# A hybrid recurrent decoder step: mixer started on the residual not yet normed, gate rows and stabiliser moved ahead of other tiles, and the third branch's division folded into its head norm

## The reference

```
rmsnorm(x, g) = x * rsqrt(mean(x*x) + 1e-6) * g
x = x + 0.5 * (silu(gate) * up) @ w_down        # gate, up = split(rmsnorm(x, g) @ w_up)
z = rmsnorm(x, mix_norm) @ w_in                 # all inputs of the three branches and their gates
x = x + (sum over branches of sigmoid(gate_c) * (o_c @ w_branch_c)) @ w_out
```

```
h = num / max(|den|, exp(-m_t))                     # one den and one m per token and head
o = h * rsqrt(mean(h*h over the head) + 1e-6) * g * sigmoid(mo)
```

## Time and profile before

| | us |
|---|---|
| median of 3 runs | 3288.1 (3286.03 to 3306.51) |
| profiled execution, whole | 3299.21 |
| its span | 3297.3 |
| PE busy in it | 3149.6 (96%) |
| mean granted TensorE clock | 0.964 of full |

### The profile page before, as it was taken

The page is one execution under the profiler, slowest core; times in us unless marked ns, Lnnn a source line. Parts: engine busy times, 40 slices in busy tenths (PEclk is TensorE's granted clock), DMA queues, the critical chain, the costliest instruction groups (busy, mean ns, idle before and its releaser), DMA issues.

```text
span 3297.3 us, 63200 instructions
## 1 busy us (share of the span) xinstructions
PE 3149.6 (96%) x23984; PEld 3044.7 (92%) x23984; DVE 1375.0 (42%) x1545; ACT 521.5 (16%) x789; POOL 1630.9 (49%) x908
## 2 busy tenths in 40 slices
PE   8999989898999999999999999989989999999998
PEld 8999989888888799999999998989888888999997
DVE  4232544535323574232642326364363254832326
ACT  2010012130231211010120101121302312110101
POOL 5555644333332366565665556533333323665655
PEclk9999989999988899999999999999999988999999
DMA  3222231131211232222222222311312122322222
GB/s 122 89 85 88 96 111 64 51 101 58 81 57 62 64 122 85 89 83 90 92 88 90 89 84 95 111 58 55 103 58 73 59 64 74 117 83 90 89 89 92
DMA packets 115154, 276.30 MB, mean 84 GB/s; under 512 B 9240, under 2 KB 53152, under 8 KB 114720
## 3 DMA queue, kind: packets, MB, share of 16 engines
q1 hardware_dynamic: 65088, 237.01, 21.6%
q10 hardware_dynamic: 49888, 36.71, 3.6%
HBM read 255.16 MB, written 18.52 MB: 83 GB/s over the span
## 4 chain that ended last, share of the span: by engine, by line
PE 85%; DVE 9%; issue 4%; ACT 1%; POOL 1%; DMA 0%; ACTq 0%; DVEq 0%; PEld 0%; POOLq 0%; PEldq 0%
PE dense L366 72%; PE SA L560 1%; PE SA L495 1%; PE SB L570 1%; PE SA L574 1%; PE SA L481 1%; PE SA L547 1%; DVE sst L1214 1%; DVE rows L1004 1%; DVE tmp L1201 1%; PE SA L424 1%; DVE vblk L1207 1%; PE SA L550 1%; POOL Wl L346 0%; PE SA L466 0%
## 5 line engine op out<-in xcount | busy, mean ns | idle before, releaser
L344 POOL TENSOR_SCALAR Wh<-raw 128x1024 fp32r<-128x1024 f32 x452 | 489.7, 1083 | 1609.9 <-PEq L371 1604.2
L346 POOL TENSOR_TENSOR Wl<-raw,Wh 128x1024 fp32r<-128x1024 f32 x452 | 1141.0, 2524 | 37.7
L366 PE MATMUL dense<-Hh,Wh 128*128 128x272 f32 x3872 | 837.7, 298 | 29.5 <-DVE Hl L913 13.4
L366 PE MATMUL dense<-Hh,Wl 128*128 128x272 f32 x3872 | 818.7, 294 | 0.0
L366 PE MATMUL dense<-Hl,Wh 128*128 128x272 f32 x3872 | 818.3, 294 | 0.0
L366 PEld LDWEIGHTS dense<-Hh,Wh 128*128 128x128 f32 x3872 | 629.3, 194 | 39.3 <-DVE Hl L926 15.2
L366 PEld LDWEIGHTS dense<-Hl,Wh 128*128 128x128 f32 x3872 | 628.9, 195 | 0.0
L366 PEld LDWEIGHTS dense<-Hh,Wl 128*128 128x128 f32 x3872 | 623.6, 195 | 0.0
L366 PE MATMUL dense<-Ah,Wh 128*128 128x272 f32 x1408 | 291.9, 289 | 6.7 <-DVE Al L948 4.2
L366 PE MATMUL dense<-Mh,Wh 128*128 128x272 f32 x1408 | 290.2, 288 | 1.8 <-DVE X L1318 1.8
L366 PE MATMUL dense<-Ml,Wh 128*128 128x272 f32 x1408 | 291.1, 288 | 0.0
(11 more groups left out here) (312 smaller groups left out, 2958.4 us busy)
## 6 DMA issues: line engine op xcount, KB each, us to landing
raw<-wst SPq DMA_DIRECT2D x452, 512.0 KB, 3.2
x_keep<-X ACTq DMA_DIRECT2D x2, 2176.0 KB, 7.8
X<-x_keep ACTq DMA_DIRECT2D x16, 272.0 KB, 3.6
sst<-st_h ACTq DMA_DIRECT2D x8, 512.0 KB, 4.1
s_h<-sst ACTq DMA_DIRECT2D x8, 512.0 KB, 3.1
sst<-st_c ACTq DMA_DIRECT2D x8, 512.0 KB, 3.9
s_c<-sst ACTq DMA_DIRECT2D x8, 512.0 KB, 3.1
X<-xT ACTq DMA_DIRECT2D x4, 544.0 KB, 7.6
```

The costliest lines, as they stand in the source:

```text
L344: pool.tensor_scalar(Wh[:, j, :], raw[:, j, :], 1.0, 0.0, ALU.mult, ALU.add).then_inc(glink, 1)
L346: pool.tensor_tensor(Wl[:, j, :], raw[:, j, :], f32(Wh[:, j, :]), ALU.subtract).then_inc(glink, 1)
L366: mm = pe.matmul(dps[slot][:, a, 0:HALF], w[:, ring, w0:w0 + 128], x[:, k, a * HALF:(a + 1) * HALF], start=(k == 0 and n == 0), stop=(k == ...
```

## The change

Three edits stand together.

1. **The seam.** In the last third of the first half-step ACT and DVE also make `Mh`/`Ml` of the residual scaled by the mixer's g (8 instructions each). PE computes tiles 0 to 3 from these, with the sum over the partitions (`rms`) behind tile 0. DVE multiplies each of the four by `rs` as it reads it out, ACT makes its sigmoid from the product, and DVE multiplies the two. The normed residual `Hh`/`Hl`, which the other tiles need, is made by DVE and ACT between these (`mix_norm`).
2. **The order.** The small tile is tile 4, directly behind `hq`; then come `hi` (5 to 8), `hf` (9 to 12) and `hg` (13 to 16). Step `rows` stands after tile 5, the stabiliser after tile 6, and `exps` and `cols` after tile 12. The first six steps of the first scan are woven with tiles 13 to 20.
3. **The third branch.** The head norm cancels a common factor of num, so the division is left out: ACT squares den and exp(-m), each scaled by sqrt(eps), squares num and copies it out; DVE takes the maximum of the two squares and adds it, capped, to num squared; the norm then has 1e-36 in place of eps. The weight of step `o` in `weave` is 5 instead of 8.

```diff
-HQ, HF, HI, HG, SMALL, GQ, GK, GV, GG = 0, 4, 8, 12, 16, 17, 19, 21, 25
+HQ, SMALL, HI, HF, HG, GQ, GK, GV, GG = 0, 4, 5, 9, 13, 17, 19, 21, 25
...
-        s += [(("o", br, h), 8 if br == 2 else 4), (("z", br, h), 8)]
+        s += [(("o", br, h), 5 if br == 2 else 4), (("z", br, h), 8)]
...
-    return (group(0, HG) + weave(group(HG, SMALL + 1), scan0[:6], 0)
-            + [("rows", 0, 0), ("stab", 0, 0)] + group(GQ, GV) + [("exps", 0, 0), ("cols", 0, 0)]
+    return (group(HQ, HI + 1) + [("rows", 0, 0)] + group(HI + 1, HI + 2) + [("stab", 0, 0)] + group(HI + 2, HG)
+            + [("exps", 0, 0), ("cols", 0, 0)]
+            + weave(group(HG, GV), scan0[:6], 0)
...
-                rms(L * 3 + 1)
...
+                        if n < SMALL:
+
+                            tile(L, n, Mh, Ml, first=(pre_lo, L * KT) if n == 0 else None)
+                            if n == 0:
+                                rms(L * 3 + 1)
+                            continue
...
+            def mix_norm(L):
+
+                def hi(k):
                     act.wait_ge(norm_h, L * KT + (k + 1))
                     act.activation(Hh[:, k, :], tmp[:, k % 2, :], ACT.Copy).then_inc(norm_hi, 1)
+
+                def sig(t):
+                    if t > 1:
+                        act.wait_ge(hq_mul, L * SMALL + (t - 1))
+                    act.wait_ge(slot_free[t % 2], ONE + L * (TILES // 2) + ((MIX_T0 + t) // 2 + 1))
+                    act.activation(tmp[:, 4 + t % 2, :], R0[0][:, t, :], ACT.Sigmoid).then_inc(sig_done, 1)
+
+                for t, ks in enumerate(((0, 1), (2, 3, 4), (5, 6, 7), ())):
+                    sig(t)
+                    for k in ks:
+                        hi(k)
...
-                    ch.did(act.activation(tmp[:, 3, 0:SEQ], SA[:, 0, :], ACT.Copy))
+                    ch.did(act.activation(tmp[:, 3, 0:SEQ], SA[:, 0, :], ACT.Square, scale=ROOT_EPS))
...
-                        act.activation(tmp[:, 5, 0:SEQ], SB[:, 0, :], ACT.Abs).then_inc(d_abs, 1)
+                        act.activation(tmp[:, 5, 0:SEQ], SB[:, 0, :], ACT.Square, scale=ROOT_EPS).then_inc(den_sq, 1)
...
+                        act.activation(tmp[:, 2, 0:SEQ], SA[:, 0, :], ACT.Square).then_inc(num_sq, 1)
...
+                    ch.did(act.activation(O[:, h, 0:SEQ], SA[:, 0, :], ACT.Copy))
...
+                dve.wait_ge(rs_ready, n + 1)
+                hq_scale(0)
+                h(0); h(1); lo(0)
+                hq_gate(0); hq_scale(1)
+                h(2); lo(1); h(3); lo(2); h(4); lo(3)
+                hq_gate(1); hq_scale(2)
+                h(5); lo(4); h(6); lo(5); h(7); lo(6); lo(7)
+                hq_gate(2); hq_scale(3)
+                hq_gate(3)
...
-                        dve.wait_ge(d_abs, (L * HEADS + h) * 2 + 2)
+
+                        dve.wait_ge(den_sq, (L * HEADS + h) * 2 + 2)
                         ch.link(TT(nb, nb, tmp[:, 5, :], ALU.max))
-                        ch.link(dve.reciprocal(nb, nb))
-                        ch.did(TT(O[:, h, 0:SEQ], SA[:, 0, :], nb[:, 0:SEQ], ALU.mult))
-                        ch.did(TT(O[:, h, SEQ:TOK], SA[:, 1, 0:SMP], nb[:, SEQ:TOK], ALU.mult))
-                        ch.sync()
-                        ch.did(TT(tmp[:, 2, :], O[:, h, :], O[:, h, :], ALU.mult))
+                        dve.wait_ge(num_sq, (L * HEADS + h) * 2 + 2)
+                        ch.link(STT(tmp[:, 2, :], nb, HUGE, tmp[:, 2, :], ALU.min, ALU.add))
```

More of the change, by code:

```diff
@@ L36 @@
 EPS = 1e-6
+ROOT_EPS = 1e-3
+TINY = 1e-36
+HUGE = 1e37
 FF_BLOCK = 8
@@ L129, in piece_of, with dram_piece @@
     return t
+def dram_piece(p):
+    i = p - MIX_P0
+    if i == SMALL:
+        return MIX_P0 + 16
+    if HI <= i < HF:
+        return MIX_P0 + 8 + i - HI
+    if HF <= i < HG:
+        return MIX_P0 + 4 + i - HF
+    if HG <= i < GQ:
+        return p - 1
+    return p - 1 if TWICE < p < FFN2_P0 else p
 class Chain:
@@ L323, in _, with run, listed @@
             with sp.Fori(0, DEPTH) as L:
-                with sp.Fori(0, TWICE // 2) as it:
-                    for j in range(2):
-                        load(L * PIECES + j + it * 2, L * PIECES + j + it * 2, j)
-                for p in range(TWICE, FFN2_P0):
-                    load(L * PIECES + p, L * PIECES + (p if p == TWICE else p - 1), p % 2)
-                with sp.Fori(0, FFN_TILES // 2) as it:
-                    for j in range(2):
-                        load(L * PIECES + (FFN2_P0 + j) + it * 2, L * PIECES + (FFN2_P0 + j) + it * 2, j)
+                def run(p0, p1):
+                    with sp.Fori(0, (p1 - p0) // 2) as it:
+                        for j in range(2):
+                            load(L * PIECES + (p0 + j) + it * 2, L * PIECES + (p0 + j) + it * 2, j)
+                def listed(p0, p1):
+                    for p in range(p0, p1):
+                        load(L * PIECES + p, L * PIECES + dram_piece(p), p % 2)
+                run(0, MIX_P0 + SMALL)
+                listed(MIX_P0 + SMALL, MIX_P0 + GQ + 1)
+                run(MIX_P0 + GQ + 1, TWICE)
+                listed(TWICE, FFN2_P0)
+                run(FFN2_P0, PIECES)
         @block.gpsimd
@@ L590, in _ @@
                     elif what == "tile":
-                        tile(L, n, Hh, Hl, first=(norm_lo, (L * 3 + 1) * KT) if n == 0 else None,
+                        if n < SMALL:
[3 more added lines that the diff above has]
+                            continue
+                        tile(L, n, Hh, Hl, first=(norm_lo, (L * 3 + 1) * KT) if n == SMALL else None,
                              part=1 if m else None)
@@ L650, in ffn, with scaled_hi @@
                         use = L * (TILES // 2) + (t0 + off + 2 * nf + m) // 2 + 1
-                        scaled_hi(Hh, m, 0, m % 2, use)
-            def scaled_hi(dst, m, g0, slot, use):
+                        scaled_hi(Hh, m, 0, m % 2, use, norm_hi)
+                else:
+                    for m in range(KT):
+                        use = L * (TILES // 2) + (t0 + off + 2 * nf + m) // 2 + 1
+                        scaled_hi(Mh, m, PG["mix"], m % 2, use, pre_hi)
+            def scaled_hi(dst, m, g0, slot, use, done):
                 act.wait_ge(slot_free[slot], ONE + use)
                 act.activation(dst[:, m, :], X[:, m, :], ACT.Copy,
-                               scale=par[:, g0 + m:g0 + m + 1]).then_inc(norm_hi, 1)
+                               scale=par[:, g0 + m:g0 + m + 1]).then_inc(done, 1)
             def tile_wait(L, t):
@@ L665, in tile @@
                 free = slot_free[slot]
-                if t in range(HQ, HF) or t in range(HG, SMALL) or t in range(GG, G0[0]):
+                if t in range(HG, GQ) or t in range(GG, G0[0]):
                     tile_wait(L, t)
@@ L670, in tile @@
                     act.activation(halves(tmp[:, t % 2, :]), ps, ACT.Sigmoid).then_inc(sig_done, 1)
-                elif t in range(HF, HI):
+                elif t in range(HF, HG):
                     tile_wait(L, t)
@@ L850, in _ @@
                     if s[0] == "tile":
-                        tile(L, s[1])
+                        if s[1] >= SMALL:
+                            tile(L, s[1])
                         if s[1] == G0[0]:
```

87 lines of the change are left out of this document (50 added, 37 removed).

## The result

The changed kernel takes **3234.06 us** (median of 4 runs, 3229.72 to 3243.32), the kernel before 3290.33 beside it (4 runs, 3286.03 to 3306.51): ratio 0.9825, 95% interval 0.9802 to 0.9847, 56 us. The profiled execution took 3236.48 us with a span of 3234.7 (3297.3 before) and a mean clock of 0.975 (0.964). The forecast was 3236.

What follows compares the result with a forecast made beforehand. PE bounds the kernel; only its time without matmuls or at half clock can be won. Seam less its cost 6.8, columns 10.6, third branch 9.0: 26.4 us a layer, 52.8 off 3288.1, say 3236 us; range 3216 to 3262.

Steps and rivals of the forecast that it cites:

- Term 1: Last third of the first half-step: eight added low parts on DVE cost 1.9 us a layer.
- Term 2: Seam, from the half-step's last matmul to the sixth tile's end: gain of 8.7 us a layer.
- The start: Seam: PE stands 2.0 us before tile 0, taken over from the other seam's 2.03.
- the stall in tile 4: Seam: PE loses 4.0 us in tiles 4 and 5, in pieces of about 1; bounds 0 and 8.
- DVE's list: Seam: 24 DVE instructions, some 0.75 us each undisturbed; those with two SBUF inputs wait for POOL's 2.74 us.
- The slower rival: Seam: DVE's list is the bound; at 2.76 us for each of 23 instructions, 3309 us; chance 0.04.
- Term 3: Rows, stabiliser and columns, sixth tile to the scan's third level: gain 10.6 us a layer, bounds 7 and 13.
- The slack of 11 us: Stabiliser ends near 496, PE's tiles 6 to 12 at 507.5, so the chain is off the path.
- Term 4: Third branch, four heads: shorter waits gain 5.4 us and clock 3.6; 9.0 a layer, bounds 1 and 16.
- I give back 3.6, one period at half clock: Third branch: of 23 us of lost clock 3.6 a layer come back, between -2 and 10.
- I take the gain from the median: Whole kernel: the 52.8 us gain is subtracted from the median 3288.1, not the profiled execution's 3299.2.
- the clock comes back too: Third branch and cols keep full clock through shorter waits: another 8 us a layer, 3219 us; chance 0.13.

Runs made afterwards that it cites:

- the kernel with the other list: Changed kernel with DVE's same 24 seam instructions reordered, readouts of tiles 2 and 3 two instructions earlier each: 3239.30 us, ratio 0.9821.
- The halves: Changed kernel with POOL's Wl made by two TENSOR_TENSOR of 512 columns instead of one of 1024: 3230.75 us, ratio 0.9803.
- The early exponentials: Changed kernel with step exps one tile earlier, before tile 12, and cols where it was: 3221.76 us, ratio 0.9770.
- the weight alone: Kernel before with step o's weight in the third branch 5 instead of 8, division kept: 3325.87 us, ratio 1.0101.
- the second trace: Trace of the changed kernel run again unaltered beside the combinations: median 3241.11 us, ratio 0.9822; the traced execution was the longest of five.

## Why the prediction was right

The time was forecast as 3236 and is 3234.06. Each edit acts where the prediction put it and by the wait that it named. That the two times are only 2 us apart is in part luck, since the half clock in the branches moves by more than that between two executions of one kernel.

- **What bounds.** PE without a matmul and PE at half clock, as said: 27.4 us of the span's 62.6 are busy time of the same matmuls.
- **Term 1** held: 35.19 us against 35.21 at the other seam, which was the same work.
- **Term 2** held in its sum (8.8 in layer 0 and 7.8 in layer 1, against 8.7). The start took 1.3 us (0.43 for POOL, 0.88 for the low part) and not 2.0, the stall in tile 4 was 2.0 and not 4.0, and in exchange a spell of half clock at its end cost 1.7, which was charged at nothing: 43.18 less 37.3 of work is 5.9, forecast 6.0. The 0.9 that waits and spell leave is the work itself: without half clock it is busy for 38.14 us (the kernel with the other list), not 37.3. DVE's list came as laid out. The rule of the Trainium skill's GPSIMD Engine Reference (section 1) agrees with the trace: products and low parts with two SBUF inputs waited for POOL, readouts of PSUM took 0.71 or 0.72 each time. The halves show that the wait lasts to the end of one POOL instruction. The slower rival, DVE's list as the bound, is out: 24 instructions took 27 us, 1.1 each.
- **Term 3** was 9.2 and 9.4, not 10.6. The wait before `cols` was forecast as 4.5 and is 4.64, 0.7 is 0.81, the wait before `rows` is gone. The clock gave 3.2 (forecast 3.6). Of the 7.0 us of waits 6.0 came: 0.25 are the two just named, and 0.76 are two waits for POOL, before 557.77 and 574.44, in tiles that are now elsewhere. The stabiliser took 5 us longer than before and ended at 501.3, not 496. Four instructions of its chain beside POOL's `Wh` and `Wl` make up the difference (1.00, 2.37, 0.95 and 2.40 us, where the same lines take 0.27, 0.15, 0.27 and 0.27 otherwise). The slack of 11 us was 6.5, and it held. The early exponentials confirm ACT as the cause of the 4.64 us.
- The table load cost 1.28 us, and the exponential behind it began 0.02 later. By the Trainium skill's "ScalarE: Activation LUTs" (What ACT_TABLE_LOAD costs) the wait would have been 5.9 us, an estimate from the forecast's 4.5 and the page's drain of 1.38; the trace decides for 4.64.
- **Term 4** was right in the waits, 5.4 and 6.3 of 5.4, and that the path and not the cover gains is shown by the weight alone (33 us slower). By place they came a little differently: before `z` in layer 0 it was 1.25, 0.53, 0.68 and 2.15 us (forecast 0.9, 2.2, 0.8 and 2.2; the second trace has 1.06, 2.06, 0.68 and 2.15), and a wait of 1.98 for the readout of a branch tile is new. The clock is where it was weak. "I give back 3.6, one period at half clock" had no row behind its size, and the four stretches that we have gave 12.5 and 4.9 in the first trace, and 7.9 and 0.0 in the second. Each of the three long waits before `z` had its own spell in the trace before, 3.4, 3.4 and 4.9 us lost. Charging them as was done before `cols`, less the one of 3.3 that stayed, would have given 8.4, near the mean of the four, 6.3. So 3.6 was low but inside what one trace can show, and so was the term: 9.0 against 17.9, 11.2, 11.5 and 4.1. The granted clock in the heads of layer 0 was 0.90 and 0.89 in the two traces (0.84 before, forecast 0.86).
- **The rival "the clock comes back too"** is right in part, for the third branch; before `cols` the clock did not come back (0.55 in the 7.6 us behind it).
- **The second branch**, which the change doesn't touch, was charged nothing and moved all the same: it lost 10.2 us of clock in each layer, where before it lost 6.8 and 11.9. Over both layers this is next to nothing. Over all kernels of this study, none of which edits that branch, it lost 3.4 to 17.1 us a layer. The cause is not settled; that it moves with the time at which the branch begins is only a guess.
- **The gain in the profile and in the time.** In the profile it is 62.6 us, 9.8 over the forecast 52.8: term 4 gave 11.1 more than forecast over both layers, the other terms 3.4 less, and places that were charged nothing gave 2.1. Between the medians it is 56.3, 3.5 over the forecast; but the kernel before, at 3290.33, was 2.2 above the 3288.1 that the sum started from, which takes most of that back. The profiled execution of the kernel before was 8.9 us above its median, that of the changed kernel 2.4. The step "I take the gain from the median" kept out of the forecast the 9 us by which the profiled execution of before lay above its median.

## What to carry to other kernels

Price a wait of the bounding engine together with the half-clock spell that the trace shows behind it, each one by its own row: in the third branch here they were worth about as much as the waits. Look at more than one layer and more than one execution before a size is read from such spells: the same code gave 0 to 12.5 us. Before shortening the work that covers a wait, take the path's own time and subtract: the same table entry was a loss of 33 us with the long path, and with the short one it made no difference that could be told. Where one engine's instruction holds up another's to its end, cutting it in two lets the other through; here it doubled PE's waits for the engine that was cut.
